# A four-layer transformer kernel: the order in which TensorE's long stages stream their tokens, and where their operands lie in SBUF

## The reference

```python
def sq_relu_mlp(h, w_up, w_down):                 # twice, D_FF = 4096
    return jnp.square(jax.nn.relu(h @ w_up)) @ w_down

def conv_ffn(h, w_up, conv_w, w_down):            # twice, D_FF_2 = 2816
    up = causal_dwconv(h @ w_up, conv_w)
    a, u = up[..., :D_FF_2], up[..., D_FF_2:]
    return (jax.nn.silu(a) * u) @ w_down
...
x = x + fox_mixer(...);  x = x + sq_relu_mlp(rms_norm(x, g), w_up, w_down)
x = x + mla_mixer(...);  x = x + sq_relu_mlp(rms_norm(x, g), w_up, w_down)
x = rms_norm(x, final_norm_g)
x = x + gla_mixer(...);  x = x + conv_ffn(rmsnorm(x, g), w_up, conv_w, w_down)
x = x + short_conv_mixer(...);  x = x + conv_ffn(rmsnorm(x, g), w_up, conv_w, w_down)
return rmsnorm(x, final_norm_g_2)
```

## Time and profile before

| | |
|---|---|
| median of 3 runs | 1189.44 us (1188.43 to 1191.84) |
| the profiled execution: its time, its span | 1188.97 us, 1187.0 us |
| mean granted clock of PE | 0.995 of 2.4 GHz |
| busy: PE, DVE, ACT, POOL | 1162.4, 873.1, 645.6, 296.3 us |
| HBM read | 201.57 MB, 171 GB/s over the span |

### The profile page before, as it was taken

How to read it: one execution, slowest core, us unless ns; L and a number is a source line. 1 busy time by engine, 2 the same in 40 slices (tenths; PEclk the granted TensorE clock), 3 DMA queues, 4 the chain that set the end, 5 groups by cost and what they waited for, 6 DMA issues and landing times.

```text
span 1187.0 us, 26180 instructions
## 1 busy us (share of the span) xinstructions
PE 1162.4 (98%) x9666; PEld 1136.4 (96%) x9666; DVE 873.1 (74%) x1383; ACT 645.6 (54%) x1055; POOL 296.3 (25%) x285
## 2 busy tenths in 40 slices
PE   6999999999999999999999999999999999999997
PEld 6998999999997999999989999999999999999997
DVE  6776777656696777755677588988767788999853
ACT  4656655544446665634455456666545455666543
POOL 4000500012230600022410263444421025444421
PEclk9999999999999999999999999999999999999999
DMA  9642655655643566465454345555556655565461
GB/s 275 208 134 96 209 177 181 204 182 177 160 137 103 163 193 194 162 210 177 143 166 155 108 142 178 178 191 166 167 186 210 208 182 178 179 198 180 149 192 59
DMA packets 212097, 203.52 MB, mean 171 GB/s; under 512 B 11824, under 2 KB 211760, under 8 KB 212032
## 3 DMA queue, kind: packets, MB, share of 16 engines
q1 hardware_dynamic: 211888, 202.44, 53.8%
q10 hardware_dynamic: 144, 0.20, 0.0%
HBM read 201.57 MB, written 1.05 MB: 171 GB/s over the span
## 4 chain that ended last, share of the span: by engine, by line
PE 94%; DVE 3%; issue 1%; ACT 1%; POOL 1%; DMA 0%; DVEq 0%; POOLq 0%; ACTq 0%
PE gemm L724 28%; PE gemm L725 28%; PE gemm L726 28%; PE gemm L735 2%; PE gemm L736 1%; PE gemm L737 1%; DVE w_lo L1604 1%; PE score L915 1%; DVE act_a L1613 1%; PE score L1030 1%; PE misc L760 0%; DMA w_raw<-in_fox_w_in 0%; PE score L1033 0%; PE score L1133 0%; PE gemm L932 0%
## 5 line engine op out<-in xcount | busy, mean ns | idle before, releaser
L1604 DVE TENSOR_TENSOR w_lo<-w_raw,w_hi 128x1024 fp32r<-128x1024 f32 (+2 forms) x404 | 483.1, 1200 | 158.5 <-ACT w_hi L1243 156.7
L1243 ACT CAST w_hi<-w_raw 128x1024 fp32r<-128x1024 f32 (+2 forms) x404 | 401.8, 999 | 172.5 <-PE gemm L726 166.8
L724 PE MATMUL gemm<-act_a,w_hi 128*128 128x256 f32 (+1 forms) x1704 | 482.2, 283 | 10.2 <-DVE act_a L1613 9.4
L725 PE MATMUL gemm<-act_a,w_hi 128*128 128x256 f32 (+1 forms) x1704 | 477.8, 280 | 0.0
L726 PE MATMUL gemm<-act_a,w_lo 128*128 128x256 f32 (+1 forms) x1704 | 477.0, 280 | 0.0
L724 PEld LDWEIGHTS gemm<-act_a,w_hi 128*128 128x128 f32 (+1 forms) x1704 | 320.7, 188 | 16.0 <-DVE w_lo L1604 9.7
L725 PEld LDWEIGHTS gemm<-act_a,w_hi 128*128 128x128 f32 (+1 forms) x1704 | 321.1, 188 | 0.4
L726 PEld LDWEIGHTS gemm<-act_a,w_lo 128*128 128x128 f32 (+1 forms) x1704 | 321.0, 188 | 0.4
L724 PE MATMUL gemm<-hid,w_hi 128*128 128x256 f32 x864 | 243.1, 281 | 0.0
L725 PE MATMUL gemm<-hid,w_hi 128*128 128x256 f32 x864 | 242.7, 281 | 0.0
L726 PE MATMUL gemm<-hid,w_lo 128*128 128x256 f32 x864 | 242.7, 281 | 0.0
(11 more groups left out here) (268 smaller groups left out, 1398.2 us busy)
## 6 DMA issues: line engine op xcount, KB each, us to landing
w_raw<-in_ffn_w_up SPq DMA_DIRECT2D x76, 1024.0 KB, 5.2
w_raw<-in_ffn_w_down SPq DMA_DIRECT2D x32, 1024.0 KB, 5.0
w_raw<-in_gla_w_in SPq DMA_DIRECT2D x12, 1024.0 KB, 5.3
w_raw<-in_ffn_w_down SPq DMA_DIRECT2D x16, 768.0 KB, 4.2
w_raw<-in_sc_w_in SPq DMA_DIRECT2D x12, 1024.0 KB, 5.1
w_raw<-in_fox_w_in SPq DMA_DIRECT2D x11, 1024.0 KB, 5.7
w_raw<-in_ffn_w_down SPq DMA_DIRECT2D x16, 640.0 KB, 3.8
w_raw<-in_fox_w_out SPq DMA_DIRECT2D x4, 1024.0 KB, 4.9
```

Source lines behind the costliest of these rows:

```text
L724: nc.tensor.matmul(ps, wh[:, k, cols], act[:, k0 + k, 0, :], start=start and k == 0, stop=False)
L725: nc.tensor.matmul(ps, wh[:, k, cols], act[:, k0 + k, 1, :], start=False, stop=False)
L1243: nc.scalar.copy(split_half(w_hi, nc_, nj), raw_half(nc_, nj)).then_inc(w_hi_ready, 1)
L1604: nc.vector.tensor_tensor(split_half(w_lo, nc_, nj), raw_half(nc_, nj), split_half(w_hi, nc_, nj).bitcast(F32), ALU.subtract).then_inc(w_l ...
```

## The change

`split_tiles` takes an argument `past`, the distance past a multiple of 128 bytes at which the tile starts (32 if not given; 80 for `act_b`, 112 for `hid`; what is not a multiple of 32 is made up by leaving out the first 4 elements of a partition). By this `act_a` stays at byte 90272, `act_b` goes to 106704, `hid` to 152304, `m_act` to 192160 (32 past a multiple of 128), and everything allocated behind `act_b` moves up by 64 bytes.

`feature_block` takes an argument `run`. Both the moving operands (high and low part) and the PSUM output then go through `in_runs`: with a positive run the 256 tokens are taken as run tokens of the first half (0 to 127), run tokens of the second half (128 to 255), the next run of the first half, and so on; with a negative one as runs in order inside, but from the last run to the first. Since operand and output are permuted alike, each token's result lands where it did. The runs: U0 16, U1 32, D1 16, CU0 8, CD0 64, CU1 -16. D0, CD1 and all other stages stay in order.

```diff
-        def split_tiles(name, n):
+        def split_tiles(name, n, past=32):
             start = used[0]
-            used[0] += (32 - start) % 64
-            return sb(name, [P, n, 2, T], F32R)
+            used[0] += (past // 32 * 32 - start) % 128
+            ahead = past % 32 // 4
+            return sb(name, [P, ahead + n * 2 * T], F32R)[:, ahead:].rearrange("p (n s t) -> p n s t", s=2, t=T)
+
+        def in_runs(ap, run):
+
+            if run is None:
+                return ap
+            if run < 0:
+                return ap.rearrange("p (i b) -> p i b", b=-run)[:, ::-1, :]
+            return ap.rearrange("p (h i b) -> p i h b", h=2, b=run)
...
-        act_b = split_tiles("act_b", KD)
+        act_b = split_tiles("act_b", KD, past=80)
...
-        hid = split_tiles("hid", DFF // P)
+        hid = split_tiles("hid", DFF // P, past=112)
...
-            def feature_block(ps, c, j, act, k0=0, col=0, start=True, stop=True, tiles=None, rows=P):
+            def feature_block(ps, c, j, act, k0=0, col=0, start=True, stop=True, tiles=None, rows=P, run=None):
...
-                last = None
+                to, last = in_runs(ps, run), None
                 for k in range(nk):
+                    hi, lo = in_runs(act[:, k0 + k, 0, :], run), in_runs(act[:, k0 + k, 1, :], run)
...
-                    nc.tensor.matmul(ps, wh[:, k, cols], act[:, k0 + k, 0, :], start=start and k == 0, stop=False)
-                    nc.tensor.matmul(ps, wh[:, k, cols], act[:, k0 + k, 1, :], start=False, stop=False)
-                    last = nc.tensor.matmul(ps, wl[:, k, cols], act[:, k0 + k, 0, :], start=False,
-                                            stop=stop and k == nk - 1)
+                    nc.tensor.matmul(to, wh[:, k, cols], hi, start=start and k == 0, stop=False)
+                    nc.tensor.matmul(to, wh[:, k, cols], lo, start=False, stop=False)
+                    last = nc.tensor.matmul(to, wl[:, k, cols], hi, start=False, stop=stop and k == nk - 1)
...
-            up("U0", AT["FO"], "ffn0")
+            up("U0", AT["FO"], "ffn0", run=16)
             down("D0", AT["U0"])
...
-            up("U1", AT["MO"], "ffn1")
-            down("D1", AT["U1"])
+            up("U1", AT["MO"], "ffn1", run=32)
+            down("D1", AT["U1"], run=16)
...
-            conv_up("CU0", AT["GO"], "ffn2")
-            conv_down("CD0", AT["CU0"])
+            conv_up("CU0", AT["GO"], "ffn2", run=8)
+            conv_down("CD0", AT["CU0"], run=64)
...
-            conv_up("CU1", AT["SO"], "ffn3")
+            conv_up("CU1", AT["SO"], "ffn3", run=-16)
             conv_down("CD1", AT["CU1"])
```

More of the change, by code:

```diff
@@ L787, in token_half, with up @@
                     last.then_inc(half_done, 2)
-            def up(stage, tiles, norm):
+            def up(stage, tiles, norm, run=None):
                 b0 = TURN[stage]
@@ L800, in up @@
                         pe.wait_ge(act_evac, AE[stage] + n - 3 + 8 * i)
-                        feature_block(gemm[b][:, 0:T], c, j, act_a, tiles=tiles if n == 0 else None).then_inc(half_done, 1)
+                        feature_block(gemm[b][:, 0:T], c, j, act_a, tiles=tiles if n == 0 else None, run=run).then_inc(half_done, 1)
                 for b in range(4):
@@ L804, in up, with down @@
                 stat(norm)
-            def down(stage, tiles):
+            def down(stage, tiles, run=None):
                 b0 = TURN[stage]
@@ L820, in down, with conv_up @@
                                           start=cc == 0, stop=cc == 3,
-                                          tiles=tiles + 8 * cc if j == 0 else None).then_inc(half_done, 1)
+                                          tiles=tiles + 8 * cc if j == 0 else None, run=run).then_inc(half_done, 1)
                 for j in range(2):
                     freed[(b0 + j) % 4] = (dve_evac, DE[stage] + 6 + j + 1)
-            def conv_up(stage, tiles, norm):
+            def conv_up(stage, tiles, norm, run=None):
                 b0 = TURN[stage]
@@ L847, in conv_up, with conv_down @@
                     freed[(b0 + n) % 4] = (dve_evac, DE[stage] + n + 1)
-            def conv_down(stage, tiles):
+            def conv_down(stage, tiles, run=None):
                 b0 = TURN[stage]
@@ L863, in body @@
                                       start=cc % 4 == 0, stop=cc % 4 == 3,
-                                      tiles=tiles + k0 if j == 0 else None).then_inc(half_done, 1)
+                                      tiles=tiles + k0 if j == 0 else None, run=run).then_inc(half_done, 1)
                 with pe.Fori(0, 3) as i:
```

## The result

The change made the kernel slower: 1196.55 us (median of 7 runs, 1194.49 to 1200.09) against 1188.52 us (7 runs) before, a ratio of 1.0059 with a 95% interval of 1.0046 to 1.0072, about 7 us (the two medians differ by 8.0). The forecast was 1175.4 us. The profiled execution took 1194.49 us, its span 1192.6.

What follows compares the result with a forecast made beforehand. PE bound by the step between matmul starts; run stages 11.7 us, hid 2.1 and m_act 0.3 sum to 14.1 us, from 1188.97 to 1174.9, plus 0.47: 1175.4 us. Range 1150 to 1196, likeliest case 1166 to 1183.

Steps and rivals of the forecast that it cites:

- What bounds the kernel: Long stages: PE busy throughout, waiting for nothing, so time is matmul count times step, 116.6 to 118.3 ns.
- The stream against the weight load: Long stages: one matmul's stream and the next's weight load conflict in SBUF at certain relative addresses, 10 to 12 ns per step.
- The four pairs: Stream and weight pairings in up, down and attention stages: step follows relative address modulo 128, 116.7 at 32, 118.3 at 96.
- the exception: CU0 stepped at 117.8 ns although its relative address was 32, where the other stages showed 116.7.
- Runs from both halves: U0, U1, D1, CU0, CD0: stream keeps the weight load's pace, steps 115.0 ns; with CU1's backward runs 11.7 us saved.
- The slower rival: Run stages: each pattern jump costs time, at most 1.6 ns, up to 1315 us; chance 0.2, a third mild, under 1200.
- deciding point: Slower rival's price per jump at which it eats the 11.7 us gain of the run stages: about 0.15 ns.
- Hid at 112: D0 and CD1, in order: hid's new address lowers the step from 118.3 to 116.7 ns, saving 2.1 us.
- Act_b at 80: 840 matmuls streaming act_b: no gain or loss counted, bounds 1.4 us either way.
- m_act: 156 matmuls streaming m_act, moved from 96 to 32 past a multiple of 128: 0.3 us saved.
- Unaligned writes: ACT and DVE writing hid's parts: at worst twice as long, 13 us of DVE in U0, nothing on the path.
- The floor of DVE in the conv stages: CU0 and CU1: step cannot fall below about 113.9 ns before PE waits for DVE to empty the banks.

Runs made afterwards that it cites:

- weights_0: all_240 with weights moved up 128 bytes, act_a at 240, act_b and hid at 112 past a multiple of 256; act_a stepped at 117.1 ns, hid 113.3; total not given.
- sides: Kernel before, addresses unchanged, runs on only the operand (U0, D0, CU0) or only the PSUM output (U1, D1, CU1); 120.0 and 123.3 against 116.6 and 117.8 ns.
- run 16: Not a separate kernel: U0's setting in the changed kernel, 16 tokens from each half in turn, against in order before; step 120.0 ns against 116.7.
- all_112: Kernel before with act_a, act_b, hid and m_act all at 112 past a multiple of 128 bytes, no runs; 1169.61 us, ratio 0.9841.
- all_240: Kernel before with act_a, act_b, hid and m_act all at 240 past a multiple of 256 bytes, no runs; 1156.85 us, ratio 0.9733.

## Why the prediction was wrong

**What bounds the kernel** was right: the long stages are count times step, nothing waits, and the difference of the times is that of the steps. "The stream against the weight load" was right in so far as the excess depends on where the stream lies against the weights (weights_0); that it is the load that gets in the way was not shown directly. The modulus was wrong, 256 and not 128. The four pairs held two relative addresses, 32 and 224, and could not tell the two rules apart. CU0, set aside as the exception, was the sign that one address can give two steps.

**The step that failed** is "Runs from both halves": that a stream which keeps pace with the weight load "nearly stops" the sweep, at 115.0 ns for these stages. The runs showed the opposite. No run below 64 was free in any place, 16 gave 120.0, 32 gave 118.7 to 120.0, 8 gave 123.3 to 124.4, 4 gave 126.7. The 11.7 us that this part should bring became +2.6, +1.5, +1.3, +5.8 and +3.5 for U0, U1, D1, CU0 and CU1, 14.7 us. Only CD0's run of 64 did no harm. The wrong modulus does not excuse it: the halves sit 512 bytes apart, a multiple of 256 too. No row had shown any order but the plain one, and I took half of a gain from an argument. Why a stream in short runs is slower stays open. The 113.3 ns that I read from single steps as the pace to be had did turn out to be the floor, but placement reached it, not order.

**The slower rival was the right one**, in its mild form: short runs cost, on the SBUF side; of the rival's two places for the price the PSUM write falls (sides). Its unit price was bounded at 1.6 ns and its deciding point put at 0.15 ns a jump; the change's act_a stages show 3.3 / 15 = 0.22 (run 16), 5.5 / 31 = 0.18 (8, from CU0's 117.8), 2.0 / 7 = 0.29 (32). But it isn't a price per jump in truth: -64 and -128 are free, -4 costs less than 4, 16 leads to the same 120.0 from 113.4 and from 118.3. Its chance stood at 0.2, a third of that for the mild form.

**Hid at 112** was right in direction and undersized: 116.7 expected, 113.4 measured, 1296 x 4.9 = 6.4 us in D0 and CD1 against 2.1 us, and 2.6 more in CD0, whose run did not spoil it. Part of it was luck: `split_tiles` fixed the place modulo 128 only, and hid happened to land at 240 and not at 112 past a multiple of 256, where all_112 stepped at 117.1. **Act_b at 80**, costed at nothing with 1.4 us either way, took about 2 us, beyond its bounds: the 118.3 to 120.0 of relative address 80. **m_act** gave some 0.2 us of the 0.3.

**Unaligned writes cost nothing on the path**, and little off it: DVE's low part of hid took 418 ns before and 418 after, ACT's high part 404 and 406. **The floor of DVE in the conv stages** was put at 113.9 ns; all_240 ran CU1 at 113.4 with PE waiting for nothing, so the floor lies a little lower, but DVE waited for PE 2.9 us in CU1 before, 6.1 in the changed kernel, and not at all in all_240. So DVE has no slack of this kind left there, and a faster PE alone would probably bring little more in CU1; no run tested that.

**What stays open**: why 112 is the good distance, what the remaining 113.3 - 106.7 = 6.6 ns are, why short runs cost, what picks one of two steps at the same address, and whether it is the load of the next matmul's weights that holds a stream up. A load taken away altogether was not tried.

## What to carry to other kernels

Where PE is busy throughout and waits for nothing, take the step from start to start stage by stage: a difference of 1.6 ns between stages of the same shape was the visible end of one of 6.7 ns (113.3 to 120.0), and moving four arrays, with no other change, was worth 2.7% (all_240). In a kernel of this shape try the fp32r stream at 112 from the weights modulo 256 first, in order or in runs of 64 and more, and judge every part of such a change by the step of its own stage, since parts of opposite sign hide each other in the total. An address rule fitted to a few pairs should be tested by moving the other operand before it is trusted.

## What the runs showed of the hardware

- The step of back-to-back fp32r matmuls of 128 x 256 at the 2.4 GHz level ran from 113.3 to 120.0 ns in order, by the relative address of stream and weights modulo 256 bytes (weights at 0 or 128), and its mean held for all of a long stage.
- The order in which a matmul reads its operand matters in runs under 64 elements (118.7 to 126.7 ns for 32 down to 4, halves in turn; 117.1 to 120.0 for runs of 32 to 4 backwards), the order in which it writes PSUM hardly (runs of 16: 116.6, of 8: 117.8).
- Moving w_lo alone held all three matmuls of a tile at 120.0 ns, and the same address could give two rhythms: 113.3 or 117.8 in different stages, 118.4 or 120.0 in the same stage of two kernels that are the same up to there.
- DMA and the splits of the weights did not matter to the step: it was 117.1 and 113.3 ns in the last 4.7 us of CD1 of all_112 and all_240, without either, as before that.
